# Inverse roots of a mixer's norms on VectorE by Newton steps in place of ScalarE's square root and a reciprocal

## What is computed

```
def modulate ... rms(x) scaled and shifted by rows worked out from a condition
q = apply_rope(rms(q) * q_gain); k = apply_rope(rms(k) * k_gain)        # per head of 64
o_attn = attention(q, k, v)
o_conv = silu(layer_norm_2(depthwise_conv31(a * sigmoid(gate)) + conv_b, ln_g, ln_b))
o = concat(rms(o_attn) * beta_attn, rms(o_conv) * beta_conv) @ w_o
x = x + g1 * o
x = x + g2 * peer(modulate(x, sh2, s2), ...)     # 8 heads x 16 experts for each token
```

## Time and profile before

| | |
|---|---|
| median of three timed runs | 3003.02 us (3002.25 to 3013.51) |
| profiled execution, own time | 3021.15 us |
| its span | 3019.3 us |
| TensorE busy | 2482.1 us, 82% |
| VectorE busy | 2113.8 us, 70%, 4458 instructions |
| ScalarE busy | 830.6 us, 28%, 2284 instructions |
| GpSimd busy | 1120.1 us, 37% |
| mean DMA rate | 344 GB/s over the span |
| Sqrt activations, L927 | 38, 11.3 us |
| table loads on L927 | 25, 32.1 us |

### The profile page before, as it was taken

The page is one execution under the profiler, slowest core; times in us unless marked ns, Lnnn a source line. Parts: engine busy times, 40 slices in busy tenths (PEclk is TensorE's granted clock), DMA queues, the critical chain, the costliest instruction groups (busy, mean ns, idle before and its releaser), DMA issues.

```text
span 3019.3 us, 27807 instructions
## 1 busy us (share of the span) xinstructions
PE 2482.1 (82%) x8610; PEld 1400.3 (46%) x8610; DVE 2113.8 (70%) x4458; ACT 830.6 (28%) x2284; POOL 1120.1 (37%) x1121
## 2 busy tenths in 40 slices
PE   6985788988888898978789777768788798788776
PEld 4663364765537566655435333323365344333322
DVE  1669669788857987877587677754374776777654
ACT  1231111000102100023444343334324343433343
POOL 1100434766543665560133333333210333333332
PEclk9997887989987899987899989999998999888999
DMA  8458998999988999970499999999830998999998
GB/s 346 174 193 336 371 393 335 384 412 412 388 352 294 386 413 412 404 297 9 169 400 418 366 420 420 416 410 388 344 115 7 370 420 362 420 419 419 415 420 338
DMA packets 183478, 1038.89 MB, mean 344 GB/s; under 512 B 26971, under 2 KB 28978, under 8 KB 99876
## 3 DMA queue, kind: packets, MB, share of 16 engines
q0 software_dynamic: 147456, 805.37, 66.3%
q1 hardware_dynamic: 35292, 230.38, 19.2%
q10 hardware_dynamic: 584, 1.36, 0.1%
HBM read 1032.60 MB, written 4.44 MB: 343 GB/s over the span
## 4 chain that ended last, share of the span: by engine, by line
PE 35%; DMA 25%; DVE 24%; issue 7%; POOL 5%; ACT 4%; another core or an unknown queue 0%; SPq 0%; ACTq 0%; DVEq 0%; POOLq 0%
PE PS L323 14%; DMA W<-in_peer_uv,IDX 14%; PE PS L2640 12%; DMA ROWS<-in_peer_uv,COEF 3%; DMA ROWS<-in_peer_uv,IDXV 3%; DVE ROWS L1334 3%; POOL ROWS L2471 3%; DVE ROWS L2264 2%; DVE W L2771 2%; DMA ROWS<-in_peer_uv,IDX 2%; PE PS L2065 2%; PE PS L2075 1%; PE PS L453 1%; DMA G<-in_peer_uv,IDX 1%; DVE PROD L2277 1%
## 5 line engine op out<-in xcount | busy, mean ns | idle before, releaser
L2640 PE MATMUL PS<-W,SCALE 128*128 128x512 f32 x1712 | 837.0, 635 | 221.6 <-ACT SCALE L2724 221.4
L2771 DVE CUSTOM_DVE_ANT_0 W<-W,PS 128x1024 f32<-128x1024 f32 x428 | 515.3, 1219 | 331.8 <-DMA W<-in_peer_uv,IDX 330.3
L2824 POOL DMA_INDIRECT W<-in_peer_uv,IDX x428 | 406.8, 950 | 685.0 <-PE PS L2640 665.9
L2640 PEld LDWEIGHTS PS<-W,SCALE 128*128 128x128 f32 x1712 | 329.1, 202 | 707.9 <-issue 706.5
L2471 POOL DMA_INDIRECT ROWS<-in_peer_uv,IDX x206 | 217.2, 1055 | 400.1 <-DVE IDX L1595 201.1
L2065 PE MATMUL PS<-XT,W 128*128 128x256 f32 x1408 | 307.3, 379 | 0.0
L2065 PEld LDWEIGHTS PS<-XT,W 128*128 128x128 f32 x1408 | 267.8, 190 | 45.5 <-issue 10.1
L2717 ACT ACTIVATE DOT<-DOT 128x1 f32<-128x1 f32 x512 | 103.6, 202 | 652.4 <-DVE DOT L2771 646.3
L323 PE MATMUL PS<-W,XT 128*128 128x512 f32 (+2 forms) x576 | 229.7, 557 | 23.9 <-issue 16.8
L323 PE MATMUL PS<-XT,W 128*128 128x128 f32 (+1 forms) x1344 | 215.4, 320 | 5.7 <-ACT XT L1047 5.7
L2724 ACT ACTIVATE SCALE<-C,COEF 128x128 f32<-128x128 f32 x512 | 205.6, 402 | 50.3 <-PE PS L2640 2.4
(11 more groups left out here) (396 smaller groups left out, 3190.7 us busy)
## 6 DMA issues: line engine op xcount, KB each, us to landing
W<-in_w_up SPq DMA_DIRECT2D x44, 1024.0 KB
W<-in_w_in SPq DMA_DIRECT2D x21, 2048.0 KB, 11.3
W<-in_w_mod SPq DMA_DIRECT2D x7, 4096.0 KB, 13.5
W<-in_w_down SPq DMA_DIRECT2D x22, 1024.0 KB
W<-in_w_o SPq DMA_DIRECT2D x6, 2048.0 KB, 8.8
W<-in_peer_wq SPq DMA_DIRECT2D x6, 2048.0 KB, 11.2
W<-in_w_out SPq DMA_DIRECT2D x4, 2048.0 KB, 10.2
W<-in_peer_uv,IDX POOLq DMA_INDIRECT x428
```

The costliest lines, as they stand in the source:

```text
L2640: ins = nc.tensor.matmul(PS[:, SUMS2[t] + h, :], SCALE[:, n % NSCALE, :], v_of(n)[:, h * 512:(h + 1) * 512], start=m == 0, stop=m == PICKS ...
L2771: nc.vector.tensor_tensor_reduce(u_of(n), u_of(n), h_of(t), 1.0, 0.0, ALU.mult, ALU.add, DOT[:, t, m:m + 1]).then_inc(s.rows_used, 1)
L2824: nc.gpsimd.indirect_dma_start(pair_slot(n), None, in_pairs, bass.IndirectOffsetOnAxis(IDX[:, t, m:m + 1], 0),).then_inc(pair_landed[fetch ...
```

## The change

The roots 2 to 7 of the context mixer and of both latent mixers, 18 in all, are worked out on VectorE alone. ScalarE's calls of `root` for them go, and so do their two semaphore waits. Roots 0, 1, 8 and 9 and those of the first block stay on ScalarE; `on_act` gives their new count on the semaphores. In the latent mixer the root of the convolution's variance is taken ahead of `maximum(9)` and not behind it, and that of the first y ahead of the wait for the gates. The second ratio needs the root itself besides its inverse, and takes it by one more reciprocal.

```diff
+RSQRT_SEED = float(0x5F3759DF)
+        def on_act(i):
+            return i + 1 if i < 8 else i - 5
-            act.wait_ge(s.stat_ready, i + 1)
+            act.wait_ge(s.stat_ready, on_act(i))
...
-                if j == 2:
-                    root(act, s, TT * 10, 2, 1.0 / HD, 1)
...
-                if i == CONV_STEP + 1:
-                    root(act, s, TT, 3, 1.0, 0)
...
-            root(act, s, TT, 4, 1.0 / CW2, 1)
...
-            root(act, s, TT, 5, 1.0 / QW, 1)
-            root(act, s, 1, 6, 1.0 / D, 1)
...
-                if t == 0:
-                    root(act, s, 1, 7, 1.0 / D, 1)
...
-            root(act, s, TT, 3, 1.0, 0)
-            root(act, s, 2, 4, 1.0 / CW2, 1)
-            root(act, s, 1, 5, 1.0 / D, 1)
-            return {4: lambda: root(act, s, 2, 6, 1.0 / CW2, 1), 7: ...
-                    11: ..., 26: ..., 27: lambda: root(act, s, 1, 7, 1.0 / D, 1),
...
-            def inverse_root(n, ins):
-                statistic(ins)
-                return inverse(cur["stat"] - 1, n)
+            def in_sum(ins):
+                link(ins)
+                cur["stat"] += 1
+            def newton(i, n, scale, e):
+                x, w, y = (a[:, i % 2, 0:n] for a in (rt, st, ri))
+                e = (LN_EPS, RMS_EPS)[e]
+                link(nc.vector.tensor_scalar(x, w, scale, e, ALU.mult, ALU.add))
+                link(nc.vector.tensor_scalar(w, x, -0.5, None, ALU.mult))
+                link(nc.vector.tensor_scalar(x.bitcast(U32), x.bitcast(U32), 1, None, ALU.logical_shift_right))
+                link(nc.vector.tensor_scalar(y.bitcast(U32), x.bitcast(U32), -1.0, RSQRT_SEED, ALU.mult, ALU.add))
+                for _ in range(3):
+                    if n == 1:
+                        link(nc.vector.scalar_tensor_tensor(x, y, y, w, ALU.mult, ALU.mult))
+                    else:
+                        link(nc.vector.tensor_tensor(x, y, y, ALU.mult))
+                        link(nc.vector.tensor_tensor(x, x, w, ALU.mult))
+                    link(nc.vector.scalar_tensor_tensor(y, x, 1.5, y, ALU.add, ALU.mult))
+                return ri[:, i % 2]
+            def inverse_root(n, ins, scale, e):
+                in_sum(ins)
+                return newton(cur["stat"] - 1, n, scale, e)
...
-            statistic(nc.vector.tensor_copy(st[:, 1, 0:TT], B["BN"][:, :, 7]))
+            in_sum(nc.vector.tensor_copy(st[:, 1, 0:TT], B["BN"][:, :, 7]))
+            r = newton(3, TT, 1.0, 0)
             maximum(9)
-            r = inverse(3, TT)
...
-            statistic(squares(B["Y"][:, 0, :], 4, 1))
+            in_sum(squares(B["Y"][:, 0, :], 4, 1))
+            r = newton(4, 2, 1.0 / CW2, 1)
+            dve.sem_inc(s.y_scale_ready, 1)
             dve.wait_ge(s.gates_loaded, 16 * 3)
             link(nc.vector.tensor_scalar(B["ROW"][2], B["ROW"][2], 1.0, None, ALU.add))
-            r = inverse(4, 2)
-            dve.sem_inc(s.y_scale_ready, 1)
...
-                r = inverse(6, 2)
+                r = newton(6, 2, 1.0 / CW2, 1)
+                link(nc.vector.reciprocal(rt[:, 0, 1:2], r[:, 1:2]))
```

More of the change, by code:

```diff
@@ L1164, in second_scores @@
                 scores_in(1, u)
-            return {4: lambda: root(act, s, 2, 6, 1.0 / CW2, 1), 7: lambda: queries_in(0, 2), 9: lambda: scores_in(0, 2),
-                    11: lambda: branch_turned("O", 1), 26: lambda: queries_in(0, 3), 27: lambda: root(act, s, 1, 7, 1.0 / D, 1),
+            return {7: lambda: queries_in(0, 2), 9: lambda: scores_in(0, 2),
+                    11: lambda: branch_turned("O", 1), 26: lambda: queries_in(0, 3),
                     29: lambda: scores_in(0, 3), 35: lambda: h_turned(1), 40: lambda: queries_in(1, 0), 47: lambda: queries_in(0, 4),
@@ L1227, in sum_squares @@
                 return ins
-            return statistic, inverse, inverse_root, sum_squares
+            return statistic, inverse, inverse_root, sum_squares, in_sum, newton
         def stream_dve_stat(dve, norms, SRC, t):
-            statistic, _, _, sum_squares = norms
+            statistic, sum_squares = norms[0], norms[3]
             statistic(sum_squares(lambda _: SRC[:, t, :], D, 1))
@@ L1256, in stream_dve_in @@
         def stream_dve_in(dve, s, link, norms, groups, B, SRC, l, latent, stage, left=False, turned=0):
-            statistic, inverse, inverse_root, sum_squares = norms
+            _, _, inverse_root, sum_squares, in_sum, newton = norms
             def left_sums():
@@ L1281, in stream_dve_in @@
             link(nc.vector.tensor_tensor(sq, q, q, ALU.mult))
-            r = inverse_root(TT * 10, nc.vector.tensor_reduce(st[:, 0, :].rearrange("p (t h) -> p t h", t=TT), sq, AX, ALU.add))
+            r = inverse_root(TT * 10, nc.vector.tensor_reduce(st[:, 0, :].rearrange("p (t h) -> p t h", t=TT), sq, AX, ALU.add), 1.0 / HD, 1)
             link(nc.vector.tensor_tensor(q, q, r[:, 0:TT * 10].rearrange("p (t h o) -> p t h o", t=TT, o=1).to_broadcast([P, TT, 10, HD]), ALU.mult))
@@ L1373, in context_mixer_dve @@
             dve.wait_ge(s.act_out_ready, 1)
-            statistic(sum_squares(lambda t: B["Y"][:, t, :], CW2))
-            inverse(4, TT)
+            inverse_root(TT, sum_squares(lambda t: B["Y"][:, t, :], CW2), 1.0 / CW2, 1)
             dve.sem_inc(s.y_scale_ready, 1)
@@ L1388, in context_mixer_dve @@
             dve.wait_ge(s.merged_ready, 1)
-            o_scale = inverse_root(TT, sum_squares(lambda t: B["O"][:, t, :], QW))
+            o_scale = inverse_root(TT, sum_squares(lambda t: B["O"][:, t, :], QW), 1.0 / QW, 1)
             dve.wait_ge(s.gates_loaded, 16 * 3)
@@ L1403, in context_mixer_dve @@
                 dve.wait_ge(s.merged_ready, 2 + t)
-                r = inverse_root(1, sum_squares(lambda _: SRC[:, t, :], D, 1))
+                r = inverse_root(1, sum_squares(lambda _: SRC[:, t, :], D, 1), 1.0 / D, 1)
                 link(nc.vector.scalar_tensor_tensor(H[:, t, :], SRC[:, t, :], r[:, 0:1], B["ROW"][2], ALU.mult, ALU.mult))
@@ L1408, in latent_mixer_dve @@
         def latent_mixer_dve(dve, s, link, norms, groups, B, SRC):
-            statistic, inverse, _, _ = norms
+            in_sum, newton = norms[4:6]
             tap_step = taps_for(s, link, B)
@@ L1454, in scaled_h @@
             def scaled_h(t, i):
-                r = inverse(i, 1)
+                r = newton(i, 1, 1.0 / D, 1)
                 link(nc.vector.scalar_tensor_tensor(H[:, t, :], SRC[:, t, :], r[:, 0:1], B["ROW"][2], ALU.mult, ALU.mult))
@@ L1488, in latent_mixer_dve @@
             onto_x(0)
-            statistic(squares(SRC[:, 0, :], 5, 0))
+            in_sum(squares(SRC[:, 0, :], 5, 0))
             scaled_h(0, 5)
@@ L1500, in second_stat @@
                 dve.wait_ge(s.act_out_ready, 2)
-                statistic(squares(B["Y"][:, 1, :], 6, 1))
+                in_sum(squares(B["Y"][:, 1, :], 6, 1))
             def second_ratio():
-                r = inverse(6, 2)
+                r = newton(6, 2, 1.0 / CW2, 1)
+                link(nc.vector.reciprocal(rt[:, 0, 1:2], r[:, 1:2]))
                 link(nc.vector.tensor_tensor(ri[:, 0, 2:3], r[:, 0:1], rt[:, 0, 1:2], ALU.mult))
@@ L1513, in second_x @@
                 onto_x(1)
-                statistic(squares(SRC[:, 1, :], 7, 0))
+                in_sum(squares(SRC[:, 1, :], 7, 0))
             return {"key": lambda: maximum(15)}, {
```

2 lines of the change are left out of this document (1 added, 1 removed).

## The result

| | before | after |
|---|---|---|
| median of 22 timed runs each, same chip | 3001.24 us (2991.93 to 3013.51) | 3010.44 us (2999.9 to 3016.75) |
| ratio, 95% interval | | 1.0024 (1.0014 to 1.0034) |
| profiled execution, span | 3021.15, 3019.3 us | 3011.31, 3009.5 us |

The change costs 7.2 us (4.2 to 10.2). The forecast had +2.7 and "same": the side and the class were right, the size was not. The two profiled executions point the other way. From the first transposes of the first block's layer 0 to those of its layer 1 (L1982), in code that the change leaves alone, before took 505.6 us and after 478.7. Over the 14 profiles of this study that stretch took 477 to 483 us or 501 to 506. Where the chip is recorded, it went with the chip and not with the kernel; before and after were caught on either side. So what follows compares stages, not spans.

The account below looks back on a forecast made before the run. It took the wait ending last at each of 18 root places to count, with HBM pacing the gather loops. 1.5 + 1.6 + 2.0 - 1.2 - 1.2 = +2.7 us on a median of 3003.02 gave some 3006 us, range 2997 to 3015.

Parts of the forecast that it names:

- Price of an instruction: VectorE's root chains: 0.20 us per linked instruction, 0.21 for 20 columns; a root 2.2, 2.6 or 2.7 us.
- Context conv root: Context mixer, conv statistic: 2.6 us between maximum and conv norm where 0.99 stood; +1.5 us reaching the Silu.
- Context x root: Context mixer, root of x, tile 0, on the chain: ten instructions take 2.2 us in place of 0.57; +1.6 us.
- q/k root of layer 0: Latent layer 0, where VectorE alone sets the pace: 2.7 us in place of 0.68 before the scaling; +2.0 us.
- Reloads: Both latent layers: the table load between the 13th and 14th Exp goes; -1.2 us in each.
- The rest at 0: Other roots, among them y, latent x of tile 0 and those in the gather loops: covered by waits or idle time, 0.
- maximum 9: Latent layer 0: slips from 1407.1 to some 1409.0 us behind the conv statistic's root, but VectorE waits for TensorE anyway; 0.
- The stage's end passes on ... so I carry +3.1 through: End of the context mixer: its delay passes on through TensorE's last query product and the next modulation weights; +3.1 us, lower bound 0.
- (a): Gather loops: their cover fails and a late dot product frees its slot late; 9.2 us added, 3015 us; chance 0.12.
- (b): Gather loops: ScalarE held the first rows, so loads and roots come off, 5.7 us a loop; 2994 us; chance 0.08.
- (c): VectorE's chains: a dependent small instruction costs 0.42 us; +32 us, 3035 us; chance 0.06.
- (d): ScalarE's table loads are all on the path: -27 us, with the additions 2979 us; chance 0.04.

Follow-up runs that it names:

- latent only: The changed file with the twelve roots of the two latent mixers on VectorE and the context mixer's on ScalarE; 1.0012 (0.9999, 1.0025) against the kernel before.
- hidden only: The changed file with only context mixer y and o and, in both latent mixers, conv statistic, y and x of tile 0 on VectorE; 1.0002 against before.
- the control: The changed file with all 18 roots back on ScalarE; 0.9989 (0.9974, 1.0004) against the kernel before.

## Why the forecast was right in side and short in size

- **Price of an instruction.** Right: 0.20 us linked, 2.10 and 2.57 us a root. For 20 columns it was low, 3.6 us and not 2.7. On VectorE's timeline of after the nine instructions of the Newton steps take 0.18 and 0.33 us by turns:

```profile
1326.26 0.18 DVE L1228 SCALAR_TENSOR_TENSOR ri<-rt,ri 128x20 f32<-128x20 f32 x1
1326.48 0.33 DVE L1226 TENSOR_TENSOR rt<-ri 128x20 f32<-128x20 f32 x1
1326.84 0.18 DVE L1227 TENSOR_TENSOR rt<-rt,st 128x20 f32<-128x20 f32 x1
1327.06 0.33 DVE L1228 SCALAR_TENSOR_TENSOR ri<-rt,ri 128x20 f32<-128x20 f32 x1
```
- **Context conv root, +1.5.** Its own part was 1.31. Missed: the y products behind it, +1.4 to +2.7.
- **Context x root, +1.6.** Its own part was 1.57. Missed: the transposes and queries behind it at half clock, +1.6 to +2.9.
- **q/k root of layer 0, +2.0.** Measured +2.9 up to the scaling behind it; at the stage's end the spells hide it (latent only +1.7, the whole change -1.7).
- **Reloads, -1.2 twice.** Right where they stand, but lost again by the 14th row of the loop, where I had carried them through to the end. The loop's loss is once more TensorE at half clock, and its transfers follow from that. The Exp now begins 0.04 us behind its maximum, where before it began 1.23 behind the earlier trace rows: the load alone. With the further 1.38 us a switch that the Trainium skill states (ScalarE: Activation LUTs, What ACT_TABLE_LOAD costs) it would have begun at some 1457.1 us before, an estimate from that page; it began at 1455.71.
- **The rest at 0.** Right for maximum 9, the y roots and the latent root of x, tile 0: hidden only, which has them all, was shorter by the reload's 1.2 us in both latent layers and level in the context mixer (87.99). The loop's roots were level again at the 38th row.
- **The step that was mis-sized.** It is "The stage's end passes on ... so I carry +3.1 through". The stage's end did pass on, but the 3.1 was 5.9 to 8.3 in the three kernels with all six roots of the context mixer on VectorE. The working took TensorE's matmuls as fixed in length and only moved their start; no term of the sum and no rival has their clock. With 5.9 to 8.3 from the context and 0 to +3 from the latent layers up to their last rows (+0.2 in after's own trace, with standard deviations of 2.3 and 1.5 us between profiles), 6 to 11 us are accounted for, and 7.2 (4.2 to 10.2) were timed.
- **Luck.** The result is in the range 2997 to 3015 because the range was as wide as the runs' own spread and as case (a), not because the half-clock time was allowed for.
- **The signs.** Chains, activations, loads and busy times came as named, and the first block starts later. The first gather was to come 1.2 us nearer to the 13th Exp; it stands 31.2 us behind it in after, 32.2 before and 30.7 in the control, so that distance tells nothing. The DMA share in the first 100 us of layer 0's loop, named as a sign of being wrong if it fell, is 0.94 in after, 0.97 before and in the control.
- **Rivals.** (a), with +11.9 at most, was no nearer to the size than the forecast, and the trace does not show its mechanism: the rows behind step 29 were level again at the 38th. (b) fell by the rows of the loop, where the two loads and the root made the fifth scaling 1.9 us sooner and no later one. (c) fell by the 0.20 us an instruction, (d) by the time itself.

## What to carry to other kernels

A small chain on VectorE in front of TensorE costs its own time and can then cost as much again, or twice that, in slower matmuls behind it. At the second place 2.44 us of idling came with 0.50 and 1.54 us did not. At the first place idle time alone does not tell: the kernel before has a spell there too, behind an idle time of 1.32 us. So when dense matmuls stand behind an exposed delay, give their clock a term of its own in the sum, and look whether a half-clock spell already ends just ahead of them. When a gain vanishes in a loop, look at the granted clock there before you blame the DMAs: the transfer that came late had waited for a product at half clock. And when a term is only 1 to 2 us, take more than one profile of each kernel.

## What the runs showed that was not expected

- TensorE, busy 12.35 of 12.5 us with small products, stayed at a granted clock of 0.50; it was back 4.5 us after 512-wide products had begun. Here spare small products did not keep the clock up.
- A change of TensorE's work ahead of the y products, be it a longer wait or spare work, cost 1.4 to 2.7 us in them, because the spell, which ended 0.2 us ahead of them in the kernel before, then reached into them.
- With the latent roots 3, 4 and 5 on VectorE, both gather loops of all four kernels had half-clock time over the product that frees the 13th gather's slot, which so came 1 to 2 us later. In the other kernels 6 loops of 20 had it.
- VectorE's instructions on 128x20 alternate between 0.18 and 0.33 us in the Newton steps; those on 1 and 2 columns take 0.15 to 0.22.
